# An attention step in a streamed encoder kernel: spare banks for the second qkv group, fewer key-sum matmuls, the decay rates moved, two weight loads halved

## What is computed

```python
def sb_attend(q, k, v, q_pos, k_pos):
    z = jnp.einsum('bqhd,bkhd->bhqk', q, k) * (SB_HEAD_DIM ** -0.5)
    mask = k_pos[None, :] < q_pos[:, None]
    log_stay = jnp.where(mask, jax.nn.log_sigmoid(-z), 0.0)
    after = lax.cumsum(log_stay, axis=3, reverse=True) - log_stay
    w = jnp.where(mask, jnp.exp(jax.nn.log_sigmoid(z) + after), 0.0)
    return jnp.einsum('bhqk,bkhd->bqhd', w, v)

def layer_forward(x, ...):
    x = x + 0.5 * swiglu(rmsnorm(x, norm_g[0]), w1g, w1u, w1d)
    y, st = mix(rmsnorm(x, norm_g[1])); x = x + y
    x = x + 0.5 * swiglu(rmsnorm(x, norm_g[2]), w2g, w2u, w2d)
    x = x + (p_i @ w_pe) * jax.nn.sigmoid(rmsnorm(x, norm_g[3]) @ w_pg)
```

## Time and profile before

| | before |
|---|---|
| median of 3 runs | 1229.05 us (1228.37 to 1229.31) |
| the profiled execution, its own time | 1229.69 us |
| its span in the trace | 1227.8 us |
| PE busy | 1188.5 us, 97% of the span |
| DVE / ACT / POOL busy | 64% / 47% / 14% |
| bytes moved | 193.20 MB, mean 157 GB/s |
| PE idle, all waits of the trace | about 30 us, in 17 pieces |
| chain that ended last | PE 85%, DVE 7%, issue 2%, ACT 2%, POOL 2%, DMA 2% |

### The profile page before, as it was taken

How to read it: one execution, slowest core, us unless ns; L and a number is a source line. 1 busy time by engine, 2 the same in 40 slices (tenths; PEclk the granted TensorE clock), 3 DMA queues, 4 the chain that set the end, 5 groups by cost and what they waited for, 6 DMA issues and landing times.

```text
span 1227.8 us, 23251 instructions
## 1 busy us (share of the span) xinstructions
PE 1188.5 (97%) x8952; PEld 1177.0 (96%) x8952; DVE 790.1 (64%) x1161; ACT 582.5 (47%) x860; POOL 177.4 (14%) x204
## 2 busy tenths in 40 slices
PE   6999999889999999999999999999996999999996
PEld 6999999889999999999999999999996999999996
DVE  7656555566649666655786666456889765665566
ACT  6444443445555444433564444344674544443353
POOL 3000011211124000002230000021245400000122
PEclk9999999899999999999999999999998999999998
DMA  6554444633343544444455444445452544444542
GB/s 221 181 171 156 145 152 165 240 104 104 104 146 138 176 166 171 150 145 162 153 191 183 155 165 149 160 148 195 147 172 88 188 171 165 152 152 143 181 145 96
DMA packets 35899, 193.20 MB, mean 157 GB/s; under 512 B 3808, under 2 KB 6128, under 8 KB 22784
## 3 DMA queue, kind: packets, MB, share of 16 engines
q1 hardware_dynamic: 34800, 187.86, 44.6%
q0 software_dynamic: 1040, 4.51, 1.1%
HBM read 188.78 MB, written 3.58 MB: 157 GB/s over the span
## 4 chain that ended last, share of the span: by engine, by line
PE 85%; DVE 7%; issue 2%; ACT 2%; POOL 2%; DMA 2%; SPq 0%; DVEq 0%; POOLq 0%; ACTq 0%
PE bank L1090 28%; PE bank L1092 27%; PE bank L1091 27%; DVE w_lo L736 2%; DMA raw<-in_up 1%; ACT w_hi L476 1%; PE bank L1135 1%; POOL sum_squares L341 1%; DVE xg_lo L745 1%; PE bank L1121 1%; DVE u_ext L868 1%; POOL gated L427 1%; DMA raw<-in_lru_o 0%; DVE y_lo L859 0%; DVE u_ext L870 0%
## 5 line engine op out<-in xcount | busy, mean ns | idle before, releaser
L476 ACT ACTIVATE w_hi<-raw 128x1024 fp32r<-128x1024 f32 (+2 forms) x410 | 370.4, 927 | 364.4 <-PE bank L1092 345.2
L736 DVE TENSOR_TENSOR w_lo<-raw,w_hi 128x1024 fp32r<-128x1024 f32 (+2 forms) x410 | 452.8, 1122 | 91.5 <-ACT w_hi L476 88.5
L1090 PE MATMUL bank<-xg_hi,w_hi 128*128 128x288 f32 x1536 | 460.1, 300 | 14.4 <-DVE w_lo L767 8.7
L1091 PE MATMUL bank<-xg_lo,w_hi 128*128 128x288 f32 x1536 | 455.6, 297 | 0.0
L1092 PE MATMUL bank<-xg_hi,w_lo 128*128 128x288 f32 x1536 | 454.1, 296 | 0.0
L1090 PEld LDWEIGHTS bank<-xg_hi,w_hi 128*128 128x128 f32 x1536 | 290.2, 189 | 17.1 <-issue 8.7
L1092 PEld LDWEIGHTS bank<-xg_hi,w_lo 128*128 128x128 f32 x1536 | 291.7, 190 | 0.0
L1091 PEld LDWEIGHTS bank<-xg_lo,w_hi 128*128 128x128 f32 x1536 | 290.9, 189 | 0.3
L1090 PE MATMUL bank<-h_hi,w_hi 128*128 128x288 f32 x704 | 208.4, 296 | 0.0
L1091 PE MATMUL bank<-h_lo,w_hi 128*128 128x288 f32 x704 | 207.7, 295 | 0.0
L1092 PE MATMUL bank<-h_hi,w_lo 128*128 128x288 f32 x704 | 207.0, 294 | 0.0
(11 more groups left out here) (186 smaller groups left out, 1275.9 us busy)
## 6 DMA issues: line engine op xcount, KB each, us to landing
raw<-in_up SPq DMA_DIRECT2D x87, 1024.0 KB, 4.8
raw<-in_down SPq DMA_DIRECT2D x64, 704.0 KB, 4.0
raw<-in_qkv SPq DMA_DIRECT2D x24, 512.0 KB, 4.4
raw<-in_ple SPq DMA_DIRECT2D x16, 640.0 KB, 3.8
raw<-in_lru_in SPq DMA_DIRECT2D x6, 1024.0 KB, 4.9
raw<-in_lru_o SPq DMA_DIRECT2D x8, 640.0 KB, 3.8
raw<-in_wo SPq DMA_DIRECT2D x4, 1024.0 KB, 4.9
raw<-in_lru_g SPq DMA_DIRECT2D x4, 1024.0 KB, 4.9
```

Source lines behind the costliest of these rows:

```text
L476: nc.scalar.activation(w_hi[slot][:, cols], raw[slot][:, cols], ACT.Copy).then_inc(w_hi_done, 1)
L736: nc.vector.tensor_tensor(w_lo[slot][:, cols], raw[slot][:, cols], w_hi[slot][:, cols].bitcast(F32), ALU.subtract).then_inc(w_lo_done, 1)
L1090: nc.tensor.matmul(out, w_hi[slot][:, cols], hi[:, k, 0:width], start=start, stop=False)
L1091: nc.tensor.matmul(out, w_hi[slot][:, cols], lo[:, k, 0:width], start=False, stop=False)
```

## The change

1. **Second qkv group.** `qkv_bank` sends group 1 to banks 4 and 5; PE no longer waits for banks 0 and 1 before it, group 2 waits for the reads of group 0, and `sum_stay(0)` for the reads of group 1.
2. **Key sums.** The columns of the score tiles are laid out anew so that what the three narrow matmuls read and add to lies side by side: a pass is one matmul of 480 columns (`LIVE`) and one of 192 (`EARLIER` from `LATER`). For that `stay_sum` gets a second half, a DVE sum of 32 columns a head behind both first halves (new semaphore `stay_live`), and `stay_high` and `stay_low` work on 512 columns and not 480. S0 is in two halves of 128, S0A and S0B, so scores and mix have two matmuls of 128 where one of 256 was.
3. **Decay rates.** `decay_rates` is cut in four parts of 5, 6, 6 and 6 instructions, behind the splits of the first four down1 groups.
4. **Seams.** The first groups of up1 and up3 are loaded as two transfers of 512 KB, each with a semaphore; in wo group 2 the splits come behind the update of `x_res` on ACT and DVE; in up1's first group PE does k 0 to 5 of both tiles and then k 6 and 7 (k 0 to 6, then 7, before).

```diff
-C0, C1, NW, S1, S0, SCOLS = 0, DEC, 2 * DEC, 3 * DEC, 3 * DEC + P, 3 * DEC + P + SEQ
+CN, NW, S1, C0, C1 = 0, DEC, 2 * DEC, 2 * DEC + P, 3 * DEC + P
+S0B, S0A, SCOLS = 4 * DEC + P, 4 * DEC + 2 * P, 4 * DEC + 3 * P
+LIVE = slice(NW, SCOLS)
+LATER, EARLIER = slice(CN, C0), slice(C0, S0A)
...
+        def qkv_bank(n, o):
+
+            return bank[4 + o] if n == 1 else bank[o]
...
+                    if phase.name in SEAMS and turn is None and n == 0:
+                        at = phase.part_a * P
+                        sp.dma_start(raw[0][:, 0:at], group_dram(phase, 0)[0, :, 0:at]).then_inc(seam_landed, 16)
+                        sp.dma_start(raw[0][:, at:2 * at], group_dram(phase, 0)[0, :, at:2 * at]) \
+                            .then_inc(raw_landed[0], 16)
...
                 for j in range(2):
                     dve.wait_ge(log_done, 2 * pair + j + 1)
-                    out = stay[pair % 2][j][:]
-                    nc.vector.scalar_tensor_tensor(out=out, in0=logit[pair % 2][j][:], scalar=0.0, in1=out,
-                                                   op0=ALU.max, op1=ALU.add).then_inc(stay_done, 1)
+                    out = stay[pair % 2][j][:, LIVE]
+                    nc.vector.scalar_tensor_tensor(out=out, in0=logit[pair % 2][j][:, LIVE], scalar=0.0, in1=out,
+                                                   op0=ALU.max, op1=ALU.add).then_inc(stay_live, 1)
+                for j in range(2):
+                    dve.wait_ge(stay_live, 2 * pair + j + 1)
+                    out = stay[pair % 2][j]
+                    nc.vector.tensor_tensor(out[:, CN:NW], out[:, C1:C1 + DEC], out[:, NW:S1], ALU.add) \
+                        .then_inc(stay_done, 1)
...
+                        if phase.name == "down1" and turn is None and n < phase.head:
+                            decay_rates(n)
...
-                        if n == 1:
-                            decay_rates()
...
-                        if n < phase.groups - 1:
+                        if n < 2:
                             part(nxt, 0)
...
-                    for s in (stay_hi[pair % 2][j], stay_lo[pair % 2][j]):
-                        opens, closes = s is stay_hi[pair % 2][j], s is stay_lo[pair % 2][j]
-                        nc.tensor.matmul(out[:, 0:SCOLS], from_here[:], s[:, 0:SCOLS], start=opens, stop=False)
-                        nc.tensor.matmul(out[:, S0 + P:S0 + SEQ], ones[:], s[:, S1:S1 + P], start=False, stop=False)
-                        nc.tensor.matmul(out[:, C0:NW], ones[:], s[:, C1:S1], start=False, stop=False)
-                        last = nc.tensor.matmul(out[:, C0:C1], ones[:], s[:, NW:S1], start=False, stop=closes)
-                    last.then_inc(summed, 1)
+                    else:
+                        pe.wait_ge((qkv_first_read, pair_free)[j], (2, QKV.first_pair + 2)[j])
+                    out, hi, lo = bank[4 + j], stay_hi[pair % 2][j], stay_lo[pair % 2][j]
+                    nc.tensor.matmul(out[:, LIVE], from_here[:], hi[:, LIVE], start=True, stop=False)
+                    nc.tensor.matmul(out[:, EARLIER], ones[:], hi[:, LATER], start=False, stop=False)
+                    nc.tensor.matmul(out[:, LIVE], from_here[:], lo[:, LIVE], start=False, stop=False)
+                    nc.tensor.matmul(out[:, EARLIER], ones[:], lo[:, LATER], start=False, stop=True) \
+                        .then_inc(summed, 1)
...
                     if kind == "qkv":
-                        if n > 0:
-                            pe.wait_ge(qkv_first_read, n)
+                        if n > 1:
+                            pe.wait_ge(qkv_first_read, n if n > 2 else 1)
...
-                        for o, ks in ((0, range(KD - 1)), (1, range(KD - 1)), (0, (KD - 1,)), (1, (KD - 1,))):
+                        early, late = (range(KD - 2), range(KD - 2, KD)) if phase.name == "up1" \
+                            else (range(KD - 1), range(KD - 1, KD))
+                        for o, ks in ((0, early), (1, early), (0, late), (1, late)):
```

More of the change, by code:

```diff
@@ L107 @@
 MASKED_OUT = -1.0e30
+SEAMS = ("up1", "up3")
 KEYS = TOK + PAST
@@ L468, in w_split @@
                 by_tile = phase.name == "qkv"
+                at_seam = phase.name in SEAMS and turn is None and n == 0
                 if by_tile and part == 0:
                     act.wait_ge(qkv_landed[slot], (n // 2 + 1) * 16)
-                if part == (1 if by_tile else 0):
+                if at_seam and part == 0:
+                    act.wait_ge(seam_landed, (SEAMS.index(phase.name) + 1) * 16)
+                if part == (1 if by_tile or at_seam else 0):
                     act.wait_ge(raw_landed[slot], loads * 16)
@@ L792, in mask_scores @@
                         dve.wait_ge(mixed, pair - 1)
-                    nc.vector.tensor_tensor(logit[pair % 2][j][:], bank[2 + j][:, 0:SCOLS], mask[:], ALU.add) \
+                    nc.vector.tensor_tensor(logit[pair % 2][j][:, LIVE], bank[2 + j][:, LIVE], mask[:, LIVE], ALU.add) \
                         .then_inc(masked, 1)
@@ L807, in exponent @@
                     dve.wait_ge(summed, 2 * pair + j + 1)
-                    out = logit[pair % 2][j][:]
-                    nc.vector.tensor_tensor(out, out, bank[4 + j][:, 0:SCOLS], ALU.subtract).then_inc(exponent_done, 1)
+                    out = logit[pair % 2][j][:, LIVE]
+                    nc.vector.tensor_tensor(out, out, bank[4 + j][:, LIVE], ALU.subtract).then_inc(exponent_done, 1)
             def v_in_rows(pair):
@@ L832, in decay_rates @@
                 e, t, z, z2, poly = (series[:, n, :] for n in (1, 2, 3, 4, 5))
[L833 to L838 removed]
+                if part == 0:
+                    dve.wait_ge(decay_act, 2)
+                    link(nc.vector.tensor_scalar(t, e, 2.0, None, ALU.add))
+                    link(nc.vector.reciprocal(t, t))
+                    link(nc.vector.tensor_tensor(z, e, t, ALU.mult))
+                    link(nc.vector.tensor_tensor(z2, z, z, ALU.mult))
+                    link(nc.vector.tensor_scalar(poly, z2, 1.0 / 17, 1.0 / 15, ALU.mult, ALU.add))
@@ L839, in decay_rates @@
+                for n in ((), (13, 11, 9), (7, 5, 3), (1,))[part]:
                     link(nc.vector.tensor_tensor(poly, poly, z2, ALU.mult))
                     link(nc.vector.tensor_scalar(poly, poly, 1.0 / n, None, ALU.add))
-                link(nc.vector.tensor_tensor(poly, poly, z, ALU.mult))
-                link(nc.vector.tensor_scalar(t, vec["lam"], -1.0, 0.0, ALU.mult, ALU.max))
-                link(nc.vector.scalar_tensor_tensor(out=t, in0=poly, scalar=2.0, in1=t, op0=ALU.mult, op1=ALU.add))
@@ L844, in decay_rates @@
-                link(nc.vector.tensor_scalar(decay[:], t, LRU_C, None, ALU.mult))
+                if part == 3:
+                    link(nc.vector.tensor_tensor(poly, poly, z, ALU.mult))
+                    link(nc.vector.tensor_scalar(t, vec["lam"], -1.0, 0.0, ALU.mult, ALU.max))
+                    link(nc.vector.scalar_tensor_tensor(out=t, in0=poly, scalar=2.0, in1=t, op0=ALU.mult, op1=ALU.add))
+                    link(nc.vector.tensor_scalar(decay[:], t, LRU_C, None, ALU.mult))
             def taps(n, tap):
@@ L1117, in scores @@
                 qkv_in_place(pe, pair, 1)
-                for at, width, key, query in ((S0, SEQ, 0, 0), (S1, P, P, P), (C0, DEC, TOK, SEQ),
+                for at, width, key, query in ((S0A, P, 0, 0), (S0B, P, 0, P), (S1, P, P, P), (C0, DEC, TOK, SEQ),
                                               (C1, DEC, TOK + P, SEQ), (NW, DEC, SEQ, SEQ)):
@@ L1161, in mix @@
                 for j, rows in enumerate(HEAD_ROWS):
-                    nc.tensor.matmul(out[rows, 0:SEQ], v[:, 0, rows], w[j][:, S0:S0 + SEQ], start=True, stop=False)
+                    nc.tensor.matmul(out[rows, 0:P], v[:, 0, rows], w[j][:, S0A:S0A + P], start=True, stop=True)
+                for j, rows in enumerate(HEAD_ROWS):
+                    nc.tensor.matmul(out[rows, P:SEQ], v[:, 0, rows], w[j][:, S0B:S0B + P], start=True, stop=False)
                 for j, rows in enumerate(HEAD_ROWS):
@@ L1241, in step @@
                     if kind == "qkv":
-                        pair = [bank[0][:, 0:TOK], bank[1][:, 0:TOK]]
+                        pair = [qkv_bank(n, o)[:, 0:TOK] for o in range(2)]
                     if kind in ("up", "qkv", "lru_in", "lru_g"):
```

40 lines of the change are left out of this document (17 added, 23 removed).

## The result

| | before | after |
|---|---|---|
| median of 4 runs each | 1229.07 us | **1215.02 us** (1214.58 to 1215.42) |
| ratio to before, 95% interval | | 0.9889 (0.9877 to 0.9901) |
| the profiled execution, and its span | 1229.69, 1227.8 us | 1214.89, 1212.8 us |
| PE busy, matmuls | 1188.5 us | 1179.7 us, 8952 |

The forecast was 1213.2 in a range of 1210.8 to 1218.0. The kernel became 14.05 us faster. The direction and nearly all terms came as predicted. 1.8 us are missing. The largest single piece is 1.5 us of low clock behind turn 7, a term that the sum had at nothing; 0.4 more is missing at up3, other terms came out 1.1 us better than reckoned, and 0.8 us comes in with the step from the profiled executions to the medians.

What follows compares the result with a forecast made beforehand. PE's queue of matmuls, with its waits and low clock, was taken as the bound. 9.3 + 1.4 + 3.5 - 0.4 - 0.5 + 0.9 + 1.0 + 0.7 = 15.9 off 1229.69, less 0.64 for the median: 1213.2 us, range 1210.8 to 1218.0.

Steps and rivals of the forecast that it cites:

- Spare banks: Before and in qkv group 1: the 3.07 us wait and 2.6 of low clock go, 5.8 us in all.
- Decay chain: Ahead of pair 0's masking in attention: moving the decay rates to down1 brings turn 1's chain forward 4.7 us.
- New stay_sum: On the stay chain ahead of turn 1: the added sums and the wait for both first halves cost 1.2 us.
- Key sums: In attention: weight loads pace passes, 0.33 us for 0.55; pairs 1 to 4 gain 3.5, less 0.4 for margins.
- rival B: In the key sums: columns pace the narrow matmuls, so the cut gains little; 1216.9 us, chance 0.05.
- Turn 7: End of attention: 0.5 us later than the stretch before, PE waits 2.5 us, pairs 5 and 6 bring nothing.
- rival A: At turn 1 or turn 7: the clock falls behind a remaining wait, 1.4 us each; 1214.6 to 1216.0, chance 0.22.
- up3: Seam into up3: with the first load now 512 KB, PE's wait of 0.72 us goes, a gain of 0.7.
- C: Middle of attention: the stay chain becomes the bound, PE waits at each turn or mix; 1216.5 to 1217.7, chance 0.16.
- E: Six later attention pairs: the chain holds PE, low clock follows each wait; slower than before, 1238 us, chance 0.03.
- F: First scores or group 3 wait for a transfer, or a bank wait remains: 1 us, 1214.2; chance 0.45 together with the forecast.
- D: Stay chain cheaper than thought: turn 7 comes 1 us sooner and no 0.4 is lost; 1211.8 us, chance 0.09.

Runs made afterwards that it cites:

- u_bank: The changed kernel with qkv group 1 back in banks 0 and 1 and the old waits for them; 1219.7 us.
- u_decay: The changed kernel with the whole decay chain back behind the splits of qkv group 1, ahead of pair 0's masking; 1220.12 us.
- b_decay: The kernel before with only the decay rates changed, in four parts behind the first down1 groups; 1222.99 us.
- u_sum: The changed kernel with three narrow matmuls (128, 32 and 32 columns) again in each key-sum pass; 1219.22 us.
- after_again: The changed kernel itself run and profiled once more, with no edit; 1214.68 us.
- e_pool: The changed kernel with GpSimd's seventh square behind up3 held back until the first lower half of the up3 weights is written; 1215.25 us.
- e_turn7: The changed kernel with the turn of pair 7's v put behind the first run of wo's tiles; 1213.6 us.

## Why the prediction came out as it did

The terms, in the prediction's order, with what the two profiled executions show:

| step | predicted | measured |
|---|---|---|
| first scores at | 237.9 | 237.89 |
| turn 1 earlier by | 9.3 (wait 1.5 stays) | 9.6 (wait 1.22) |
| clock behind turn 1 | 1.4 | 1.5 |
| key sums, pairs 1 to 4, less margin | 3.1 | 3.4 |
| turn 7 against the stretch before it | -0.5 | -0.1 |
| clock behind turn 7 | 0 | **-1.5** |
| pair 7's sum | 0.9 | 0.9 |
| up1 seam | 1.0 | 1.0 |
| up3 seam | 0.7 | **0.3** |
| sum | 15.9 | 15.1 (the spans differ by 15.0) |

- **Spare banks, right.** PE goes from the mean through group 1 without idle time and at full clock; both transfers that could have been late were in time. u_bank loses the 3.2 of wait again; the clock's part was 2.6 before and 1.6 in u_bank, so that part of the 5.8 depends on the execution.
- **Decay chain, right,** from both sides: 5.1 by u_decay, 6.2 by b_decay. More than the 4.7, since with the chain in place a longer wait stands at turn 1 and the clock falls behind it.
- **New stay_sum, right in the main.** Two sums of 32 columns in 0.31 us and ACT's 0.90 of idle time in front of stay_high (246.16, 256.27) are what was expected; the chain came 0.3 earlier than reckoned.
- **Key sums, right.** Passes of 0.33 by the pace of the weight loads; rival B falls with u_sum. The extra score and mix matmul a head cost nothing visible: u_sum has them and takes 30.05 us for the three groups where the kernel before takes 30.01 (274.82 to 304.83). The 0.4 taken off for margins did not happen.
- **Turn 7, size off.** I had the mechanism (splits of 3.30 beside stay_lo, stay_high of pair 6 ahead of the splits), but a wait of 2.5, and it was 1.95.
- **Clock behind turn 7: the step that failed.** The sum carried no price for the clock behind a wait that it had itself forecast at 2.5 us; rival A named the case, with a price of 1.4 and a chance of 0.22. Measured 1.5; in all, 1.3 to 1.5 in six of eight profiled executions with that wait. A wait of 2.5 stood nearer to the 2.46 that had dropped the clock than to the 1.61 that had not, and the 2.76 near 940 that had kept it spoke the other way. So half the price or all of it belonged in the sum, which gives 1213.9 to 1214.6.
- **up3, size off.** The load did come earlier (the first split starts 0.8 sooner against PE), but the forecast left out what POOL does beside that split. In after_again and e_pool, where DVE begins before POOL, PE doesn't wait at up3.
- **Rivals.** A came true at turn 7 and not at turn 1; its range, 1214.6 to 1216.0, holds the result. B, C, E and F fell. D named a cheaper chain: the overlap on POOL is there (splits of 3.30 and 3.33), so its cause fell, but two of its effects came in part, no 0.4 lost and turn 7 0.4 sooner. (The low end of C's range, 1216.5, is 0.3 under what its terms give.) 1215.02 against 1213.2 is 1.5 of clock and 0.4 at up3, less 0.3 at the chain, 0.1 of clock behind turn 1, 0.3 of margin and 0.4 at turn 7, which makes 0.8; of the other 1.0, 0.8 lies in the medians (the profiled execution of before was 0.6 above its median, that of after 0.1 below) and the rest outside the spans. That the forecast came this close is in part luck: the sum was 1.9 us too hopeful in two terms and 1.1 too cautious in four others.

Two things stay open. One is what the unprofiled executions of e_turn7 did, whose median is 1.4 lower where the stretch shows 2.3. In the profiled one 0.4 of the 2.3 goes between the first group of up1 and the last matmul, 0.3 of it from lru_o to up3, where its clock fell at 925 and the changed kernel's had not; the rest of the way to the spans' 1.4 is a mean that starts 0.15 later and 0.35 behind the last matmul. The other is how often the clock falls in executions that no trace shows.

## What to carry to other kernels

Whoever forecasts that a wait of about 2 us stays on TensorE should price the low clock behind it, as a chance times some 1.5 us (less where TensorE is held by its weights a few us later, as in lru_o), and compare two kernels by stretches between fixed points, not by spans, since such falls come and go at places that the edit doesn't touch. When several narrow matmuls of this kind (fp32r, 128x128 weights) each need a load, count loads at 0.11 us and not columns: laying the columns side by side so that one matmul does the work of three took 0.22 us off each pass, 0.87 a pair. Before sending more work to GpSimd, or more in front of a split, look which of GpSimd and VectorE begins first where such instructions overlap: here the later one paid, and it should not be the one that TensorE waits for.

## What was not expected of the hardware

- The clock's fall behind a wait is not settled by the wait's length: it fell behind waits of 1.91 to 3.12 us and not behind others of 1.67 to 2.77, at one place of one kernel family. One fall cost 1.3 to 1.6 us where it stood, behind 3.07 us 1.6 in u_bank and 2.6 in the kernel before, and behind 4.32 us 2.7.
- VectorE and GpSimd stretch each other by order of arrival. A split of 2.36 us takes 3.3 when stay_lo began before it, and stay_lo, 2.53, takes 3.26 when the split began first; at up3 1.23 becomes 1.75, or 0.81 becomes 1.67. The Trainium skill, GPSIMD Engine Reference, 8. Key points, says that GpSimd shares its SBUF interfaces with VectorE and contends with VectorE instructions of two SBUF inputs. The trace agrees, with w_lo reading two tensors. That the one that comes second pays is read from these rows.
